# Conditioning product in eight halves of four column tiles over the first four feed-forward chunks, and loops over one chunk

## The chip, the cores and the metric

The kernel runs on one core of one Trainium2 chip. The metric is the device time of one execution in microseconds (us), as the median of several runs. Five engines work side by side: TensorE (PE; its weight loads are shown as PEld), VectorE (DVE), ScalarE (ACT), GpSimd (POOL) and SyncE (SP), which here issues nearly all DMA loads. Each engine works off its own instructions in program order, and they wait for each other on semaphores.

## The reference

One step of a decoder layer for a prompt of 1024 tokens and 8 samples of one token each, in float32, model width 1024, feed-forward width 2816. What matters here is the conditioning product `mod` and the first feed-forward:

```python
mod = (jax.nn.silu(c) @ w_ada[l] + b_ada[l]).reshape(c.shape[0], 9, 1, D_MODEL)
h = x * (1 + mod[:, 1]) + mod[:, 0]
x = layer_norm(ALPHA * x + 0.5 * mod[:, 2] * swiglu(h, ffn1_wg[l], ffn1_wu[l], ffn1_wd[l]),
               ln_g[l, 0], ln_b[l, 0])
h = x * (1 + mod[:, 4]) + mod[:, 3]
out, k_a, v_a, k_b, v_b = mixer(l, h)
x = layer_norm(ALPHA * x + mod[:, 5] * out, ln_g[l, 1], ln_b[l, 1])
h = x * (1 + mod[:, 7]) + mod[:, 6]
x = layer_norm(ALPHA * x + 0.5 * mod[:, 8] * swiglu(h, ffn2_wg[l], ffn2_wu[l], ffn2_wd[l]),
               ln_g[l, 2], ln_b[l, 2])
```

`c` has 9 rows (one of the prompt, eight of the samples); `w_ada` is 1024 x 9216, 37.7 MB.

## The kernel before

**The two feed-forwards** each run over 11 chunks of 256 hidden columns. Tokens (1032) are in three groups `g` of 344 columns; every product is three float32r matmuls (`mm3`, L211 to L213: high times high, high times low, low times high). A chunk has an **up phase** of six units (0 to 5), each of which is gate and up for one half `j` of the chunk and one group `g`, 48 matmuls, in the order (0,0), (0,1), (0,2), (1,0), (1,1), (1,2), and a **down phase** of 24 outputs of 6 matmuls.

**Behind a unit** stand ACT's SiLU into SIL (L393), DVE's product with the up bank into GF (L427), ACT's rounded copy Ghi (L399) and POOL's remainder Glo (L472). The units share two pairs of PSUM banks: PE may start unit u when GF of unit u-2 is done (the wait on `gf_done` in `up_pe`, L348).

**Weights** come in six pieces of 0.5 MB for each chunk (two of wg, two of wu, two of wd) through three buffers RAW, fetched by SP in order (`ffn_fetch_chunk`, L305). Piece q may be fetched when piece q-3 has been split. ACT splits off the high part (`split_hi`, L309, waits for the landing) and POOL the low part (L313). ACT does this at two places of its program (`refill_after`): the next chunk's pieces 0 and 1 between unit 2's and unit 3's work, pieces 2 to 5 after unit 5.

**The conditioning product** is cut in 18 blocks of 512 columns. Blocks 0 to 3 are done before the first feed-forward, two column tiles wide (`ada4_*`). Blocks 4 to 17 are done inside it, in groups of three blocks with bases 4, 7, 10, 13 and 15 (block 15 twice). For each block 32 columns of `siluT` are the stationary operand, and the three blocks of a group go to three column tiles of 32 output rows of one PSUM bank. A group is done in two **halves** of the contraction (four of eight k tiles each). SP fetches a half as three loads of 1 MB into ADA0 to ADA2 (`ada_fetch`, L531), each after PE has done the half before (`ada_done`); `ada_pe` (L541) does 12 matmuls. After a group's second half comes its **turn**: DVE copies the bank to `modrow` (L556), PE transposes it in four pieces (L550), and DVE adds `b_ada` into `modT` (L517).

**Where the halves stand.** In `ffn_pe` a chunk with one half does it after unit 5, before the down phase; a chunk with two does the first after unit 2 and the second after unit 5. Chunk 0 has two halves (group 0, which the down phase of chunk 0 needs); chunks 1 to 8 have one each; 9 and 10 none. SP fetches them in the matching places: a half's loads stand behind the weight pieces of its chunk.

**Loops.** On PE and DVE chunks 1 to 6 are a loop (`Fori`) of three passes over a body of two chunks; 7 to 10 are written out. ACT and POOL loop over one chunk. The second feed-forward has on all engines a loop over one chunk (PE's at L1984), without conditioning.

SP also loads, behind the first half of group 1, `bias_rows` (1.5 MB) and `joint_rows` (4.5 MB).

Of the kernel before, what the change touches and what calls it, by code (L numbers as in the profile page):

```python
# [9 lines left out]
P = 128  # L10
# [11 lines left out]
CH = FT // 2  # L22
# [10 lines left out]
UNIT_D = NG * KT  # L33

F32 = mybir.dt.float32
# [79 lines left out]
def build(nc, io):  # L115

    ctx = ExitStack()
    with ctx:
        arena = Arena(nc)

        def sem(name):
            return ctx.enter_context(nc.semaphore(name))
# [24 lines left out]
        ident = arena.at("ident", [P, P], F32, off); off += 4 * P  # L147
# [28 lines left out]
        LNOFF = off  # L176
        ADA = []
        o = LNOFF
        for i in range(3):
            ADA.append(arena.at(f"ADA{i}", [P, KT // 2, 512], F32, o)); o += 2 * KT * 512  # L180
        o = LNOFF
        NT = []
# [3 lines left out]
        for g in range(NG):  # L186
# [6 lines left out]
        o = HOFF + 4 * TB * D + 4 * D + 8 * P  # L193
        ADA4 = [arena.at("ADA4_0", [P, KT, 512], F32, o), arena.at("ADA4_1", [P, KT, 512], F32, LNOFF),
                arena.at("ADA4_2", [P, KT, 512], F32, LNOFF + 16384), arena.at("ADA4_3", [P, KT, 512], F32, GOFF)]
        modrow = arena.at("modrow", [96, 512], F32, LNOFF + 32768)
        TABLES = o + 16384
        OUTT = [arena.at(f"OUTT{i}", [P, D], F32, HOFF + 4 * D * i) for i in range(4)]

# [3 lines left out]
        bank = [psum[:, i, :] for i in range(8)]  # L203
        MISC = 7
# [12 lines left out]
        x_in = [sem(f"x_in{h}") for h in range(2)]  # L217
        setup_pe, setup_act, setup_dve = sem("setup_pe"), sem("setup_act"), sem("setup_dve")
        ada4_in = [sem(f"ada4_in{i}") for i in range(4)]
        ada_in = [sem(f"ada_in{i}") for i in range(3)]  # L220
        ada_done, ada_evac, ada_turned = sem("ada_done"), sem("ada_evac"), sem("ada_turned")
        ada4_done = sem("ada4_done")
        mod_prep = sem("mod_prep")
# [29 lines left out]
        ffn = {1: FFN(1), 2: FFN(2)}  # L253
# [71 lines left out]
        def ffn_fetch_chunk(sp, x, c, slots=range(6)):  # L325
            for s in slots:
                fetch(sp, f"ffn{x.n}", x.source(2 * c, s), 6 * c + s, s % 3, 2 * c + s // 3)


        FULL = [(0, 0), (0, 1), (0, 2), (1, 0), (1, 1), (1, 2)]  # L330
# [109 lines left out]
        def ffn_dve(dve, x, r, ub, db, units, ada=(), before=None, norm=None, down0=0, done=0):  # L440

            for i in range(done, len(units)):
                if before is not None and (not done and i < NG):
                    norm_y(dve, before, i)
                gf_dve(dve, x, ub + i, i)
                if before is not None and done and i <= NG:
                    norm_y(dve, before, i - 1)
            turns = ada and ada[-1][2]
            if turns:
                ada_dve(dve, ada[-1][0])  # L450
            if len(ada) == 2:
                ada_turn_dve(dve, *ada[-1][:2])
                dve.wait_ge(ada_evac, 2 * ada[-1][0] + 7)
                prep_gate(dve, 2, 0.5)
            for g in range(len(units) // 2):
                if before is not None:
                    dve.wait_ge(ln_y, before.at(g))
                if norm is not None and g == 2:
                    center(dve, norm, 0)
                for d in range(KT):  # L460
                    v = KT * g + d
                    if norm is not None and v == 2 * KT + 4:
                        center(dve, norm, 1)
                    down_dve(dve, x, db + v, d, g, bank[4 + (down0 + v) % 3])
                    if norm is not None:
                        two_sums(dve, g, d, x.y_evac, db + v + 4)
                    if d == 2 and g == 0 and turns and len(ada) == 1:
                        ada_turn_dve(dve, *ada[-1][:2])

        def g_lo_pool(pool, x, u, i, j, g):  # L470
# [40 lines left out]
        def mod_add(dve, first, blocks):  # L511

            out = modT[:, bass.ds(4 * first, 4 * blocks), :].rearrange("p (i j) n -> p i j n", j=4)
            bias = vecT[:, bass.ds(4 * first, 4 * blocks)].rearrange("p (i j) -> p i j", j=4)
            turned = bank[MISC][:, 0:128 * blocks].rearrange("p (j i n) -> p i j n", j=4, i=blocks)[:, :, :, 0:NC1]
            for i in range(blocks):
                last = dve.tensor_tensor(out[:, i], turned[:, i], bias[:, i].unsqueeze(2).to_broadcast([P, 4, NC1]),  # L517
                                         ALU.add)
            last.then_inc(ada_evac, 1)
# [6 lines left out]

        def ada_fetch(sp, base, q, half):

            for i in range(3):
                sp.wait_ge(ada_done, 3 * q + i + 1)  # L530
                sp.dma_start(ADA[i][:, :, :], wada[:, 4 * half:4 * half + 4, bass.ds((base + i) * 512, 512)]  # L531
                             ).then_inc(ada_in[i], 16)

        def ada_pe(pe, group, base, half):
            if half == 0:
                pe.wait_ge(ada_evac, 2 * group + 5)
            for i in range(3):
                pe.wait_ge(ada_in[i], 32 * group + 16 * half + 16)
            for k in range(4):
                for i in range(3):  # L540
                    ins = pe.matmul(bank[MISC][32 * i:32 * i + 32, :], siluT[:, 4 * half + k, :], ADA[i][:, k, :],  # L541
                                    start=(half == 0 and k == 0), stop=(half == 1 and k == 3))
                    if k == 3:
                        ins.then_inc(ada_done, 1)

        def ada_turn_pe(pe, group):

            pe.wait_ge(ada_evac, 2 * group + 6)
            for j in range(4):
                last = pe.transpose(bank[MISC][:, 96 * j:96 * j + 96], modrow[:, j * P:(j + 1) * P],  # L550
                                    ident[0:96, 0:96])
            last.then_inc(ada_turned, 1)

        def ada_dve(dve, group):
            dve.wait_ge(ada_done, 6 * group + 9)
            dve.tensor_copy(modrow[:, :], bank[MISC][0:96, :]).then_inc(ada_evac, 1)  # L556

        def ada_turn_dve(dve, group, base):
            dve.wait_ge(ada_turned, group + 3)
            mod_add(dve, base, 3)  # L560

        def mod(i):
            return modT[:, i * KT:(i + 1) * KT, :]
# [1010 lines left out]
        def _(sp):  # L1574
# [26 lines left out]
            ada_fetch(sp, 4, 0, 0)  # L1601
            ada_fetch(sp, 4, 1, 1)
            ffn_fetch_chunk(sp, ffn[1], 1)
            ada_fetch(sp, 7, 2, 0)
            sp.wait_ge(bias_out, 80)
            sp.dma_start(bias_rows, bass.AP(bias_heads.tensor, 3 * NH * EXT, [[0, P], [1, NH * EXT]])).then_inc(bias_spread, 16)
            sp.dma_start(joint_rows, bass.AP(joint_heads.tensor, 0, [[0, P], [1, NH * EXTA]])).then_inc(bias_spread, 16)
            ffn_fetch_chunk(sp, ffn[1], 2)
            ada_fetch(sp, 7, 3, 1)
            with sp.Fori(2, 4) as g:  # L1610
                ffn_fetch_chunk(sp, ffn[1], 2 * g - 1)
                ada_fetch(sp, 3 * g + 4, 2 * g, 0)
                ffn_fetch_chunk(sp, ffn[1], 2 * g)
                ada_fetch(sp, 3 * g + 4, 2 * g + 1, 1)
            for half in range(2):
                ffn_fetch_chunk(sp, ffn[1], 7 + half)
                ada_fetch(sp, 15, 8 + half, half)
            with sp.Fori(9, CH) as c:
                ffn_fetch_chunk(sp, ffn[1], c)
            after_phase(sp, "proj")  # L1620
            for q in range(6):
# [190 lines left out]
        def _(dve):  # L1812
# [13 lines left out]
            for k in range(3):  # L1826
                last = dve.tensor_copy(BROWJ[:, k * EXT:(k + 1) * EXT], bank[k][0:2 * NH, 0:EXT])
# [8 lines left out]
                scaled(dve, init, g)  # L1836
                input_lo(dve, init, g)
            ffn_dve(dve, ffn[1], 0, 0, 0, FULL, ((0, 4, 0), (0, 4, 1)), before=init)
            with dve.Fori(1, 4) as g:
                ffn_dve(dve, ffn[1], 2 * g - 1, 6 * (2 * g - 1), UNIT_D * (2 * g - 1), FULL, ((g, 3 * g + 4, 0),))  # L1840
                ffn_dve(dve, ffn[1], 2 * g, 6 * (2 * g), UNIT_D * (2 * g), FULL, ((g, 3 * g + 4, 1),))
            for c in (7, 8):
                ffn_dve(dve, ffn[1], c, 6 * c, UNIT_D * c, FULL, ((4, 15, c - 7),))
            ffn_dve(dve, ffn[1], 9, 54, 9 * UNIT_D, FULL)
            dve.wait_ge(ada_evac, 15)
            prep(dve, 3, 4, 0)
            ffn_dve(dve, ffn[1], CH - 1, 6 * (CH - 1), UNIT_D * (CH - 1), FULL, norm=ln[1])
            dve.wait_ge(ffn[1].y_evac, UNIT_D * CH + 3)
# [59 lines left out]
        def _(pe):  # L1908
            for n in (1, 2):
                pe.sem_inc(ffn[n].up_done, 6)  # L1910
                pe.sem_inc(ffn[n].down_done, UNIT_D)
            pe.sem_inc(ada_done, 3)
            pe.wait_ge(const_ready, 4)
            pe.wait_ge(rows_in, 80)
            nv = MT + 6 * KT
# [4 lines left out]
            for u in range(XU):  # L1920
# [5 lines left out]
                for b in range(4):  # L1926
                    last = pe.transpose(bank[2 + u % 4][:, b * P:(b + 1) * P],
                                        XTOK[:, 4 * h + b, k * P:(k + 1) * P], ident[:, :])
# [15 lines left out]
            ada4_pe(pe, 1)  # L1944
            pe.wait_ge(bias_ev, 1)
            ffn_pe(pe, ffn[1], 0, 0, 0, FULL, ((0, 4, 0), (0, 4, 1)), fresh=True)
            with pe.Fori(1, 4) as g:
                ffn_pe(pe, ffn[1], 2 * g - 1, 6 * (2 * g - 1), UNIT_D * (2 * g - 1), FULL, ((g, 3 * g + 4, 0),))
                ffn_pe(pe, ffn[1], 2 * g, 6 * (2 * g), UNIT_D * (2 * g), FULL, ((g, 3 * g + 4, 1),))
            for c in (7, 8):  # L1950
                ffn_pe(pe, ffn[1], c, 6 * c, UNIT_D * c, FULL, ((4, 15, c - 7),))
            ffn_pe(pe, ffn[1], 9, 54, 9 * UNIT_D, FULL)
            ffn_pe(pe, ffn[1], CH - 1, 6 * (CH - 1), UNIT_D * (CH - 1), FULL, norm=ln[1])
            var_pe(pe, ln[1], 0)
            pe.wait_ge(resid_done, 1)
# [67 lines left out]
```

## Time and profile before

| | us |
|---|---|
| median of 3 runs | 2281.07 |
| the runs | 2275.48, 2281.56, 2281.07 |
| the profiled execution | 2280.34 |
| its span, first to last instruction | 2278.5 |
| PE busy | 2171.7 (95%) |
| DVE busy | 800.7 (35%) |
| POOL busy | 624.1 (27%) |
| ACT busy | 568.0 (25%) |

The chain of work that ended last, followed back from the last instruction, is PE for 87% and DVE for 7% of the span. The first feed-forward lies between about 56 and 882 us, the second between about 1468 and 2240 us. The views are of one execution; times in them count from the span's start. In a row of the timeline stand the start, the length, engine, line, operation, what is written from what, the shape, and in brackets how long the engine was idle before it and what ended that. "issue" there is idle time for which the profile shows no wait.

### The profile page before, as it was taken

The numbers are of one execution on the slowest core, as the hardware profiler recorded it, in microseconds if no ns is written. First come the engines' busy times: TensorE is split into PE (matmuls) and PEld (weight loads), VectorE is DVE, ScalarE is ACT, GpSimd is POOL, SyncE is SP. The second block draws the span as 40 slices with busy tenths as digits, with TensorE's granted clock in tenths as the row PEclk, the third lists the DMA queues.
The fourth block names the chain that finished last, engine by engine and source line by source line (L and its number), as shares of the span: only waits on it lengthen the run. The fifth ranks groups of instructions, "written<-read, shape, count | busy, mean of one in ns | idle before, by whom it ended". The sixth has DMA issues, their size and how long they took to land.

```text
span 2278.5 us, 33154 instructions
## 1 busy us (share of the span) xinstructions
PE 2171.7 (95%) x13244; PEld 1990.6 (87%) x13244; DVE 800.7 (35%) x1763; ACT 568.0 (25%) x1072; POOL 624.1 (27%) x397
## 2 busy tenths in 40 slices
PE   6999999999999999999789889989999999999996
PEld 2899999999999997998644459889999999999995
DVE  1432212321123339102455652762222212222228
ACT  2211121111111114322355550351111121111114
POOL 1422232223232230133233342132323232323210
PEclk8999999999999999999989999999999999999999
DMA  8463213222121020422442012111111111111001
GB/s 287 158 203 111 93 38 111 93 93 88 61 95 54 28 56 1 157 62 88 143 140 84 1 38 65 38 38 56 45 48 50 42 47 45 54 38 55 28 1 75
DMA packets 167775, 171.36 MB, mean 75 GB/s; under 512 B 14235, under 2 KB 130699, under 8 KB 167157
## 3 DMA queue, kind: packets, MB, share of 16 engines
q1 hardware_dynamic: 167668, 169.84, 23.0%
q8 instruction: 80, 1.31, 0.2%
q14 instruction: 27, 0.21, 0.0%
HBM read 156.91 MB, written 19.20 MB: 77 GB/s over the span
## 4 chain that ended last, share of the span: by engine, by line
PE 87%; DVE 7%; SPq 2%; ACT 2%; issue 1%; DMA 1%; POOL 0%; DVEq 0%; ACTq 0%
PE psum L211 26%; PE psum L213 25%; PE psum L212 25%; PE psum L1075 2%; PE psum L541 2%; PE psum L1134 1%; PE psum L976 1%; PE psum L639 1%; PE psum L1431 1%; SPq L494 1%; DVE NT L690 1%; DVE Hlo L703 1%; DVE RSTD L671 1%; PE psum L968 1%; DVE Y L654 1%
## 5 line engine op out<-in xcount | busy, mean ns | idle before, releaser
L211 PE MATMUL psum<-Hhi,Whi 128*128 128x344 f32 x2736 | 882.9, 323 | 26.7 <-DVE GF L427 9.9
L213 PE MATMUL psum<-Hhi,Wlo 128*128 128x344 f32 x2736 | 878.8, 321 | 0.0
L212 PE MATMUL psum<-Hlo,Whi 128*128 128x344 f32 x2736 | 878.2, 321 | 0.0
L313 POOL TENSOR_TENSOR Wlo<-RAW,Whi 128x1024 fp32r<-128x1024 f32 x158 | 393.1, 2507 | 690.4 <-ACT Whi L309 689.7
L211 PEld LDWEIGHTS psum<-Hhi,Whi 128*128 128x128 f32 x2736 | 519.2, 190 | 37.4 <-issue 22.5
L213 PEld LDWEIGHTS psum<-Hhi,Wlo 128*128 128x128 f32 x2736 | 518.9, 190 | 0.0
L212 PEld LDWEIGHTS psum<-Hlo,Whi 128*128 128x128 f32 x2736 | 518.2, 189 | 0.3
L427 DVE TENSOR_TENSOR GF<-SIL,psum 128x344 f32<-128x344 f32 x132 | 67.7, 513 | 898.3 <-ACT SIL L393 898.2
L434 DVE SCALAR_TENSOR_TENSOR Y<-psum,G,Y 128x344 f32<-128x344 f32 (+1 forms) x528 | 300.9, 572 | 181.4 <-PE psum L213 181.4
L211 PE MATMUL psum<-Ghi,Whi 128*128 128x344 f32 x1056 | 341.4, 323 | 9.8 <-DVE Y L434 5.3
L212 PE MATMUL psum<-Glo,Whi 128*128 128x344 f32 x1056 | 338.8, 321 | 0.0
L213 PE MATMUL psum<-Ghi,Wlo 128*128 128x344 f32 x1056 | 338.1, 320 | 0.0
L472 POOL TENSOR_TENSOR Glo<-GF,Ghi 128x344 fp32r<-128x344 f32 x132 | 125.8, 953 | 725.1 <-ACT Ghi L399 725.1
L309 ACT ACTIVATE Whi<-RAW 128x1024 fp32r<-128x1024 f32 x158 | 159.5, 1048 | 521.0 <-PE psum L213 461.2
L393 ACT ACTIVATE SIL<-psum 128x344 f32<-128x344 f32 x132 | 60.3, 457 | 692.0 <-PE psum L213 692.0
L211 PEld LDWEIGHTS psum<-Ghi,Whi 128*128 128x128 f32 x1056 | 198.5, 188 | 19.5 <-issue 7.5
L213 PEld LDWEIGHTS psum<-Ghi,Wlo 128*128 128x128 f32 x1056 | 199.5, 189 | 0.0
L212 PEld LDWEIGHTS psum<-Glo,Whi 128*128 128x128 f32 x1056 | 199.0, 188 | 0.4
L1075 PEld LDWEIGHTS psum<-ident,SLOT 128*128 128x128 f32 x408 | 47.8, 151 | 55.0 <-POOL SLOT L1063 29.8
L399 ACT ACTIVATE Ghi<-GF 128x344 fp32r<-128x344 f32 x132 | 65.0, 492 | 87.2 <-DVE GF L427 86.3
L1075 PE MATMUL psum<-ident,SLOT 128*128 128x128 f32 x408 | 66.7, 302 | 18.4 <-POOL SLOT L1063 10.3
L1063 POOL TENSOR_SCALAR SLOT<-SLOT,U_RDEN 128x128 f32<-128x128 f32 (+7 forms) x64 | 47.0, 748 | 82.7 <-DVE U_RDEN L1048 82.7
(196 smaller groups left out, 1309.3 us busy)
## 6 DMA issues: line engine op xcount, KB each, us to landing
ADA<-in_w_ada SPq DMA_DIRECT2D x38, 1024.0 KB, 9.2
RAW<-in_ffn_wg SPq DMA_DIRECT2D x44, 512.0 KB, 3.9
RAW<-in_ffn_wu SPq DMA_DIRECT2D x44, 512.0 KB, 3.7
RAW<-in_ffn_wd SPq DMA_DIRECT2D x44, 512.0 KB, 3.7
RAW<-in_w_in SPq DMA_DIRECT2D x36, 256.0 KB, 3.4
SK<-in_cache_a_k SPq DMA_DIRECT2D x24, 256.0 KB, 3.4
SK<-in_cache_a_v SPq DMA_DIRECT2D x24, 256.0 KB, 3.8
joint_rows<-joint_heads SPq DMA_DIRECT2D x1, 4608.0 KB, 28.0
```

Of the source, the lines that this page charges most:

```text
L211: pe.matmul(out, whi, xhi, start=first, stop=False)
L212: pe.matmul(out, whi, xlo, start=False, stop=False)
L213: return pe.matmul(out, wlo, xhi, start=False, stop=last)
L309: act.activation(Whi[slot][:, :, :], RAW[raw][:, :, :], ACT.Copy).then_inc(W[phase].hi, 1)
L313: pool.tensor_tensor(Wlo[slot][:, :, :], RAW[raw][:, :, :], Whi[slot][:, :, :].bitcast(F32), ALU.subtract).then_inc(W[phase].ready, 1)
L393: act.activation(SIL[i % 2][:, :], bank[2 * (i % 2)][:, 0:TG], ACT.Silu).then_inc(x.silu_done, 1)
L399: act.activation(Ghi[j][:, group(g)], GF[i % 2][:, :], ACT.Copy).then_inc(x.g_hi, 1)
L427: dve.tensor_tensor(GF[i % 2][:, :], SIL[i % 2][:, :], bank[2 * (i % 2) + 1][:, 0:TG], ALU.mult).then_inc(x.gf_done, 1)
L434: last = dve.scalar_tensor_tensor(Y[:, d, cols], bk[:, 0:n], G9[:, d, 0:1], Y[:, d, cols], ALU.mult, ALU.add)
L472: pool.tensor_tensor(Glo[j][:, group(g)], GF[i % 2][:, :], Ghi[j][:, group(g)].bitcast(F32), ALU.subtract).then_inc(x.g_ready, 1)
L1063: pool.tensor_scalar(s, s, U_RDEN[:, u % 3, e:e + 1], 1.0, ALU.mult, ALU.mult).then_inc(normed, 1)
L1075: last = pe.transpose(bank[4 + p % 2][:, j * P:(j + 1) * P], slot(u, e)[:, c:c + P], ident[:, :])
```

## The change

The conditioning product inside the first feed-forward is done in groups of four blocks, with bases 4, 8, 11 and 14 (blocks 11 and 14 are computed twice). A fourth buffer ADA3 is added; `modrow` and the transposes are 128 rows wide. There are four groups of two halves, 16 matmuls and four loads of 1 MB in each. All eight halves are in chunks 0 to 3, two in each chunk, so that chunks 1 to 3 have the form that only chunk 0 had. PE and DVE loop over one chunk: one loop over chunks 1 to 3 with two halves and a turn, one over chunks 4 to 9 without. SP's loops follow this. Between SP's fetch of a chunk's weight pieces and that of the next chunk's now stand both halves' loads.

```diff
-        for i in range(3):
+        for i in range(4):
             ADA.append(arena.at(f"ADA{i}", [P, KT // 2, 512], F32, o)); o += 2 * KT * 512
...
-        modrow = arena.at("modrow", [96, 512], F32, LNOFF + 32768)
+        modrow = arena.at("modrow", [P, 512], F32, LNOFF + 32768)
...
-            if len(ada) == 2:
+            if turns and isinstance(r, int) and r == 0:
+
                 ada_turn_dve(dve, *ada[-1][:2])
-                dve.wait_ge(ada_evac, 2 * ada[-1][0] + 7)
+                dve.wait_ge(ada_evac, 7)
                 prep_gate(dve, 2, 0.5)
...
-                    if d == 2 and g == 0 and turns and len(ada) == 1:
+                    if d == 2 and g == 0 and turns and not (isinstance(r, int) and r == 0):
                         ada_turn_dve(dve, *ada[-1][:2])
...
-            for i in range(3):
-                sp.wait_ge(ada_done, 3 * q + i + 1)
+            for i in range(4):
+                sp.wait_ge(ada_done, 4 * q + i + 1)
                 sp.dma_start(ADA[i][:, :, :], wada[:, 4 * half:4 * half + 4, bass.ds((base + i) * 512, 512)]
                              ).then_inc(ada_in[i], 16)
...
-            for i in range(3):
+            for i in range(4):
                 pe.wait_ge(ada_in[i], 32 * group + 16 * half + 16)
             for k in range(4):
-                for i in range(3):
+                for i in range(4):
                     ins = pe.matmul(bank[MISC][32 * i:32 * i + 32, :], siluT[:, 4 * half + k, :], ADA[i][:, k, :],
...
-                last = pe.transpose(bank[MISC][:, 96 * j:96 * j + 96], modrow[:, j * P:(j + 1) * P],
-                                    ident[0:96, 0:96])
+                last = pe.transpose(bank[MISC][:, 128 * j:128 * j + 128], modrow[:, j * P:(j + 1) * P], ident[:, :])
...
             ffn_fetch_chunk(sp, ffn[1], 1)
-            ada_fetch(sp, 7, 2, 0)
+            ada_fetch(sp, 8, 2, 0)
             sp.wait_ge(bias_out, 80)
...
-            ffn_fetch_chunk(sp, ffn[1], 2)
-            ada_fetch(sp, 7, 3, 1)
-            with sp.Fori(2, 4) as g:
-                ffn_fetch_chunk(sp, ffn[1], 2 * g - 1)
-                ada_fetch(sp, 3 * g + 4, 2 * g, 0)
-                ffn_fetch_chunk(sp, ffn[1], 2 * g)
-                ada_fetch(sp, 3 * g + 4, 2 * g + 1, 1)
-            for half in range(2):
-                ffn_fetch_chunk(sp, ffn[1], 7 + half)
-                ada_fetch(sp, 15, 8 + half, half)
-            with sp.Fori(9, CH) as c:
+            ada_fetch(sp, 8, 3, 1)
+            with sp.Fori(2, 4) as c:
+                ffn_fetch_chunk(sp, ffn[1], c)
+                ada_fetch(sp, 3 * c + 5, 2 * c, 0)
+                ada_fetch(sp, 3 * c + 5, 2 * c + 1, 1)
+            with sp.Fori(4, CH) as c:
                 ffn_fetch_chunk(sp, ffn[1], c)
...
-            with pe.Fori(1, 4) as g:
-                ffn_pe(pe, ffn[1], 2 * g - 1, 6 * (2 * g - 1), UNIT_D * (2 * g - 1), FULL, ((g, 3 * g + 4, 0),))
-                ffn_pe(pe, ffn[1], 2 * g, 6 * (2 * g), UNIT_D * (2 * g), FULL, ((g, 3 * g + 4, 1),))
-            for c in (7, 8):
-                ffn_pe(pe, ffn[1], c, 6 * c, UNIT_D * c, FULL, ((4, 15, c - 7),))
-            ffn_pe(pe, ffn[1], 9, 54, 9 * UNIT_D, FULL)
+            with pe.Fori(1, 4) as c:
+                ffn_pe(pe, ffn[1], c, 6 * c, UNIT_D * c, FULL, ((c, 3 * c + 5, 0), (c, 3 * c + 5, 1)))
+            with pe.Fori(4, CH - 1) as c:
+                ffn_pe(pe, ffn[1], c, 6 * c, UNIT_D * c, FULL)
```

DVE's loops change in the same way as PE's, and `ada_dve`, `ada_turn_dve` and `mod_add` take four blocks.

SP, from the first half of chunk 1 on, before. RAW0 and RAW1 with `wg` and `wu` are pieces 0 and 1 of chunk 2:

```order
L531 DMA ADA0_87<-in_w_ada 128x4x512
L531 DMA ADA1_88<-in_w_ada 128x4x512
L531 DMA ADA2_89<-in_w_ada 128x4x512
L1606 DMA bias_rows<-bias_heads 128x3072
L1607 DMA joint_rows<-joint_heads 128x9216
L305 DMA RAW0_56<-in_ffn1_wg 128x8x128
L305 DMA RAW1_57<-in_ffn1_wu 128x8x128
L305 DMA RAW2_58<-in_ffn1_wg 128x8x128
```

And the same place now, with the start of SP's loop over chunks 2 and 3:

```order
L1606 DMA bias_rows<-bias_heads 128x3072
L1607 DMA joint_rows<-joint_heads 128x9216
L532 DMA ADA0_87<-in_w_ada 128x4x512
L532 DMA ADA1_88<-in_w_ada 128x4x512
L532 DMA ADA2_89<-in_w_ada 128x4x512
L532 DMA ADA3_90<-in_w_ada 128x4x512
L1609 UNCONDITIONAL_BRANCH
L1609 ISA
L305 ISA
L305 DMA RAW0_56<-in_ffn1_wg 128x8x128
L304 REGISTER_ALU
L305 DMA RAW1_57<-in_ffn1_wu 128x8x128
```

The loads of chunk 1's second half, four instead of none, now stand between the bias rows and pieces 0 and 1 of chunk 2.

PE, at the end of unit 2 and the start of unit 3 (weights `Whi2_79`) in chunk 1, before:

```order
L213 MATMUL psum<-Hhi_50,Wlo1_55 128x344
L371 REGISTER_ALU
L348 REGISTER_ALU
L211 MATMUL psum<-Hhi_50,Whi2_79 128x344
L212 MATMUL psum<-Hlo_51,Whi2_79 128x344
```

And the end of the half that now stands there, with its last five matmuls of 16:

```order
L542 MATMUL psum<-ADA3_90,siluT_63 32x512
L542 MATMUL psum<-ADA0_87,siluT_63 32x512
L542 MATMUL psum<-ADA1_88,siluT_63 32x512
L542 MATMUL psum<-ADA2_89,siluT_63 32x512
L542 MATMUL psum<-ADA3_90,siluT_63 32x512
L371 REGISTER_ALU
L348 REGISTER_ALU
L211 MATMUL psum<-Hhi_50,Whi2_79 128x344
L212 MATMUL psum<-Hlo_51,Whi2_79 128x344
```

A first half has moved between units 2 and 3, where before the units followed each other.

## Rows read from the trace of the kernel before

**Rows 1.** The page, its first line and PE's busy time.
```profile
span 2278.5 us, 33154 instructions
...
PE 2171.7 (95%) x13244; PEld 1990.6 (87%) x13244; DVE 800.7 (35%) x1763; ACT 568.0 (25%) x1072; POOL 624.1 (27%) x397
```

**Rows 2.** Chain of waits, 80 to 900 us: start, length, work.
```profile
87.76 3.65 PE psum L541 x24
...
260.72 3.56 PE psum L541 x24
...
336.62 3.56 PE psum L541 x24
...
408.28 3.56 PE psum L541 x24
...
483.94 3.56 PE psum L541 x24
...
555.61 3.56 PE psum L541 x24
...
627.64 3.56 PE psum L541 x24
```

**Rows 3.** PE's loop lines: durations ns min/median/max, first and last start us.
```profile
L1947 PEldq COMPARE_BRANCH  x3: 83/3535/3692, 285.5 to 580.4; - x3
...
L1984 PEldq COMPARE_BRANCH  x9: 83/215/237, 1619.7 to 2163.0; - x9
```

**Rows 4.** Timeline of PEld, conditioning batches two tiles wide.
```profile
49.06 0.11 PEld L502 LDWEIGHTS psum<-ADA,siluT 128*32 128x32 f32 x2 [0.32 <-issue]
49.49 0.11 PEld L502 LDWEIGHTS psum<-ADA,siluT 128*32 128x32 f32 x2 [0.32 <-issue]
```

**Rows 5.** Timeline of PE; then windows: PE busy, PEclk, DMA share, GB/s.
```profile
436.90 0.42 PE L211 MATMUL psum<-Hhi,Whi 128*128 128x344 f32 x1 [1.81 <-issue]
...
1498.32 0.42 PE L211 MATMUL psum<-Hhi,Whi 128*128 128x344 f32 x1 [1.70 <-DVE GF L427]
...
437.40:440.60 3.20, 3.20 (x13) 0.51 0.18 51
1498.40:1502.00 3.60, 3.60 (x23) 1.00 0.68 199
```

**Rows 6.** DMA packets, 290 to 433 us; 1640 to 2150 us, whose only queue this is.
```profile
q8 instruction: 7, 0.11, 0.3%
...
q1 hardware_dynamic: 32430, 23.52, 15.0%
```

**Rows 7.** Timeline of ACT and PE in chunk 0.
```profile
103.59 1.06 ACT L309 ACTIVATE Whi<-RAW 128x1024 fp32r<-128x1024 f32 x1 [14.27 <-DMA RAW<-in_ffn_wg]
105.45 1.06 ACT L309 ACTIVATE Whi<-RAW 128x1024 fp32r<-128x1024 f32 x1 [0.81 <-DMA RAW<-in_ffn_wu]
106.42 0.44 ACT L393 ACTIVATE SIL<-psum 128x344 f32<-128x344 f32 x1
...
107.45 0.43 PE L211 MATMUL psum<-Hhi,Whi 128*128 128x344 f32 x1 [0.86 <-DVE GF L427]
```

**Rows 8.** SP's loads by line: chunk 0's halves, two pieces, then a loop's half.
```profile
L531 SPq DMA_DIRECT2D ADA<-in_w_ada x3: 378/505/507, 76.5 to 77.4; - x3
...
DMA to landing us min/median/max: 5.0/7.6/9.7
...
L531 SPq DMA_DIRECT2D ADA<-in_w_ada x3: 368/505/507, 91.3 to 92.3; - x3
...
DMA to landing us min/median/max: 5.0/7.3/9.5
...
L305 SPq DMA_DIRECT2D RAW<-in_ffn_wu x1: 4456/4456/4456, 93.6 to 93.6; - x1
...
DMA to landing us min/median/max: 10.7/11.2/11.8
...
DMA to landing us min/median/max: 8.2/10.2/12.3
```

More of the change, by code:

```diff
@@ L219, in build @@
         ada4_in = [sem(f"ada4_in{i}") for i in range(4)]
-        ada_in = [sem(f"ada_in{i}") for i in range(3)]
+        ada_in = [sem(f"ada_in{i}") for i in range(4)]
         ada_done, ada_evac, ada_turned = sem("ada_done"), sem("ada_evac"), sem("ada_turned")
@@ L549, in ada_turn_pe @@
             for j in range(4):
-                last = pe.transpose(bank[MISC][:, 96 * j:96 * j + 96], modrow[:, j * P:(j + 1) * P],
-                                    ident[0:96, 0:96])
+                last = pe.transpose(bank[MISC][:, 128 * j:128 * j + 128], modrow[:, j * P:(j + 1) * P], ident[:, :])
             last.then_inc(ada_turned, 1)
         def ada_dve(dve, group):
-            dve.wait_ge(ada_done, 6 * group + 9)
-            dve.tensor_copy(modrow[:, :], bank[MISC][0:96, :]).then_inc(ada_evac, 1)
+            dve.wait_ge(ada_done, 8 * group + 12)
+            dve.tensor_copy(modrow[:, :], bank[MISC]).then_inc(ada_evac, 1)
         def ada_turn_dve(dve, group, base):
             dve.wait_ge(ada_turned, group + 3)
-            mod_add(dve, base, 3)
+            mod_add(dve, base, 4)
         def mod(i):
@@ L1838, in _ @@
             ffn_dve(dve, ffn[1], 0, 0, 0, FULL, ((0, 4, 0), (0, 4, 1)), before=init)
-            with dve.Fori(1, 4) as g:
-                ffn_dve(dve, ffn[1], 2 * g - 1, 6 * (2 * g - 1), UNIT_D * (2 * g - 1), FULL, ((g, 3 * g + 4, 0),))
-                ffn_dve(dve, ffn[1], 2 * g, 6 * (2 * g), UNIT_D * (2 * g), FULL, ((g, 3 * g + 4, 1),))
-            for c in (7, 8):
-                ffn_dve(dve, ffn[1], c, 6 * c, UNIT_D * c, FULL, ((4, 15, c - 7),))
-            ffn_dve(dve, ffn[1], 9, 54, 9 * UNIT_D, FULL)
-            dve.wait_ge(ada_evac, 15)
+            with dve.Fori(1, 4) as c:
+                ffn_dve(dve, ffn[1], c, 6 * c, UNIT_D * c, FULL, ((c, 3 * c + 5, 0), (c, 3 * c + 5, 1)))
+            with dve.Fori(4, CH - 1) as c:
+                ffn_dve(dve, ffn[1], c, 6 * c, UNIT_D * c, FULL)
+            dve.wait_ge(ada_evac, 13)
             prep(dve, 3, 4, 0)
@@ L1911, in _ @@
                 pe.sem_inc(ffn[n].down_done, UNIT_D)
-            pe.sem_inc(ada_done, 3)
+            pe.sem_inc(ada_done, 4)
             pe.wait_ge(const_ready, 4)
@@ L1946, in _ @@
             ffn_pe(pe, ffn[1], 0, 0, 0, FULL, ((0, 4, 0), (0, 4, 1)), fresh=True)
-            with pe.Fori(1, 4) as g:
-                ffn_pe(pe, ffn[1], 2 * g - 1, 6 * (2 * g - 1), UNIT_D * (2 * g - 1), FULL, ((g, 3 * g + 4, 0),))
-                ffn_pe(pe, ffn[1], 2 * g, 6 * (2 * g), UNIT_D * (2 * g), FULL, ((g, 3 * g + 4, 1),))
-            for c in (7, 8):
-                ffn_pe(pe, ffn[1], c, 6 * c, UNIT_D * c, FULL, ((4, 15, c - 7),))
-            ffn_pe(pe, ffn[1], 9, 54, 9 * UNIT_D, FULL)
+            with pe.Fori(1, 4) as c:
+                ffn_pe(pe, ffn[1], c, 6 * c, UNIT_D * c, FULL, ((c, 3 * c + 5, 0), (c, 3 * c + 5, 1)))
+            with pe.Fori(4, CH - 1) as c:
+                ffn_pe(pe, ffn[1], c, 6 * c, UNIT_D * c, FULL)
             ffn_pe(pe, ffn[1], CH - 1, 6 * (CH - 1), UNIT_D * (CH - 1), FULL, norm=ln[1])
```

## The prediction

> **What bounds the kernel now.** The page's busy times come first: PE is busy for 95% of a span of 2278.5 us [rows 1]. The profiled execution took 2280.34 us, 1.8 us more than its span; the median of the runs is 2281.07 us, 0.7 us above it. I make the sum against 2280.34. The change lies in the first eleven-chunk feed-forward, so the next view is the chain of waits there. The conditioning pieces (L541) sit in it at a regular distance [rows 2], and that gives every price of a chunk. From 483.94 to 555.61 lies a chunk with one conditioning half: 71.67 us. From 555.61 to 627.64 lies one that also turns a group: 72.03 us. From 260.72 to 336.62 and from 408.28 to 483.94 lie a turn and the jump back of the loop over two chunks: 75.90 and 75.66 us. The second feed-forward, whose loop body is one plain chunk, has eight jumps in 2163.0 - 1619.7 us [rows 3]: 67.91 us a chunk. So on PE's path **a half costs 71.67 - 67.91 = 3.76 us, a turn 0.36 us, a jump of the two-chunk loop 3.87 and 3.63 us**. In these chunks PE waits for nobody; what the other engines do costs nothing until it makes PE wait.
>
> **What the change does to the halves.** Before, ten halves with three column tiles each; after, eight with four. In one batch, the matmuls for all tiles start within some nanoseconds, and the next batch follows after 0.43 us. Two tiles wide, the batches stand at 49.06 and 49.49 [rows 4]; three wide, eight batches take 3.56 us, 0.44 us each [rows 2]. Width cost nothing between two and three, so I take it as free at four: a half stays at 3.76 us. Two halves and one turn fewer: 2 x 3.76 + 0.36 = **-7.9 us**. The upper bound is a fourth tile that costs a third of a batch, 0.14 us in each of 64 batches, 9.2 us. The 128-wide copy of modrow and the fourth addition to modT lie on DVE, for which PE waits only in chunk 0's turn; I take 0.1 us there and nothing in the others, whose 0.36 us is the price of a turn with three additions.
>
> **The jumps.** PE's branch at L1947 (body of two chunks) took 3.5 and 3.7 us when taken, the one at L1984 (body of one chunk) 0.2 us [rows 3]. The first makes PE idle for 1.8 us and then costs clock: after 1.81 us of idle time before 436.90 the granted clock was 0.51 (1.2 GHz) for 3.2 us; after 1.70 us before 1498.32 it stayed at 1.00 (2.4 GHz) [rows 5]. So 3.63 - 1.81, about **1.8 us, is what a drop of the clock costs**. I take the same for the other jump. The DMA view says why the jumps differ: while the two-chunk loop ran, instruction packets were loaded (7 in 143 us), while the one-chunk loop ran, none [rows 6]. The new loop's body has 432 matmuls and 32 for the conditioning plus 4 transposes, near the 432 of the cheap body and far from the 892 of the dear one. I take it as cheap. It has two jumps, the plain loop behind it five cheap ones. The two dear jumps go: **-7.5 us**; bounds 0 and -7.5.
>
> The Trainium skill (Runtime: NRT & Kernel Launch, Instruction fetch mechanics) says that a taken branch whose target is outside a window of two 256-instruction pages stops for a fetch. By that rule all seven jumps of the new loops would cost like the two of before. The cheap branch at L1984 jumps over a body of 864 weight loads and matmuls, more than two such pages, so the trace disagrees.
>
> **What the change does to the queue of loads.** This is what decides. In each of chunks 0 to 3 both halves are done, the first after up unit 2, the second after unit 5. Both use the same buffers, so SP waits for PE's first half before it issues the second half's four loads, and the first two weight pieces of the next chunk stand behind them. ACT is to split those two pieces after unit 2, in program order ahead of the SiLU of unit 3, and PE's unit 5 needs the bank that this SiLU and GF free. Before, only chunk 0 is like this, and the trace shows the result: ACT idle for 14.27 us until the first piece, then the second piece, the split from 105.45, the SiLU at 106.42, and PE's unit 5 at 107.45 after 0.86 us idle [rows 7]. The loads: issued from 91.3 us, the first landed after 5.0 us, the third (issued at 92.3) after 9.5, so one megabyte takes (92.3 + 9.5 - 91.3 - 5.0) / 2 = 2.7 us; the second piece landed at 93.6 + 11.8 = 105.4 us [rows 8], just when ACT starts on it. A fourth tile puts 2.7 us more ahead of it. PE then idles 0.86 + 2.7 = 3.6 us before unit 5, and such a gap brings the clock drop: 1.8 us.
> - Chunk 0: 2.7 + 1.8 = 4.5 us (its 0.86 is in the time before).
> - Chunks 1 to 3: 3 x (3.6 + 1.8) = 16.2 us.
> - The first half of chunk 0: its third tile landed at 77.4 + 9.7 = 87.1 us [rows 8], PE came at 87.76 [rows 2]. The fourth lands at 89.8: 2.1 us idle, and 1.8 us for the clock: 3.9 us.
> - In chunks 2 and 3 the loads are issued in SP's loop, with registers. There a first load landed after 8.2 us instead of 5.0 [rows 8]; that one had a weight piece ahead of it, others did not suffer as much. Bounds 0 and 3.2 us each; I take 1: 2.0 us.
>
> Together **+26.6 us**. The rest is covered. 432 matmuls in 71.67 - 3.56 us are 0.158 us each, so an up unit of 48 takes 7.6 us and a down phase of 144 takes 22.7. The first halves of chunks 1 to 3 are loaded from early in the down phase before, over 40 us ahead of their use, and four loads need 5.0 + 3 x 2.7 = 13.1 us. The second halves have three units, 22.7 us, for the same. The 6.1 MB of bias rows, issued behind the first half of chunk 1, need 17 us at that rate (double that would still end before the second half is asked for).
>
> **Sum.** -7.9 - 7.5 + 26.6 + 0.1 = +11.3 us. Since the two clock prices of chunk 0 may overlap with the slow stretch the start already has, I take off half a microsecond: +10.8, or 2291 us.
>
> **Rivals.**
> - *The jumps stay dear.* The new body is 8% longer than the cheap one. If it no longer fits, two jumps cost 3.75 us each: 2298.5 us. For it: nothing in the trace lies between 432 and 892 matmuls. Against: the distances.
> - *No clock drop.* If the five new gaps leave the clock at 1.00, 5 x 1.8 us fall away: 2282 us, within 0.3%, which is what a measurement of this kernel can tell from no change. For it: the 1.70 us gap did not; against: all five come out longer than 2 us.
> - *Faster: the weight pieces don't queue.* If the transfers ran side by side, so that the two pieces landed within 12 us of the first issue, unit 5 would start on time in all four chunks. That takes away 4 x 5.4 and the 2.0: 2267.5 us. It decides from about 13 us on: unit 5 was due at 107.45 - 0.86 = 106.6, 15.3 us after the first issue, and starts 2.1 us after the landing. Against: the landings came one after the other in the order of issue [rows 8].
> - *The fourth tile isn't free*: 9.2 us, 2300 us.
> - *Every jump stops PE*, the page's rule as a mechanism of this kernel: five jumps more at 3.75 us, and the two stay, so 7 x 3.75 = 26.3 us: 2317 us. The trace speaks against it by eight cheap jumps.
>
> **Chances.** The forecast as costed 0.67, and about 0.05 of that lies under 2288 us; dear jumps 0.10; no clock drop 0.12; faster 0.07; fourth tile 0.03; every jump 0.01. Slower by over 0.3%: 0.62 + 0.10 + 0.03 + 0.01 = 0.76; within: 0.12 + 0.05 = 0.17; faster: 0.07. The range takes in the forecast, the dear jumps and the case without clock drop, with 2 us for errors of the terms: 2280 to 2301.
>
> **What would show it.** In the profile after: four waits of PE's L211 for DVE's GF of about 3.6 us, one in each of chunks 0 to 3, each behind an ACT wait of 15 to 18 us for a weight piece; a clock of 0.50 for some 3 us after each; a wait of about 2 us for the conditioning load at 88 us; taken branches of 0.2 us and no wait of L211 for "issue"; 3.56 us for each of eight conditioning pieces. Waits under 2 us, or landings of the second piece under 15 us from the first issue, make the prediction wrong towards no change or faster; branches of 3.5 us towards slower.

## The result, and the profile after

The changed kernel takes 2290.49 us (median of 6 runs, 2289.3 to 2294.0), the kernel before 2277.6 us on the same chips. The ratio is 1.0064 (95% interval 1.005 to 1.0078): 0.64% slower. Timed again beside others it was 1.0068 (1.0054 to 1.0082). The forecast was 2291 us. One run of two_chunk_body below (2689.0 us at a mean granted clock of 0.75) and one of the kernel before in a later group (3057.4 us at 0.65) stand apart as slow runs, and medians and ratios here are without them.

PE's waits in the first feed-forward: who waited for whom, total, times, longest. The kernel before, 90 to 850 us, all lines:

```profile
PE psum L211 <- issue: 3.8, 2, 2.0
PE psum L211 <- DVE Y L434: 2.4, 2, 1.5
PE psum L211 <- DVE GF L427: 0.9, 1, 0.9
```

The changed kernel, 60 to 850 us, all lines:

```profile
PE psum L211 <- DVE GF L427: 20.5, 5, 5.5
PE psum L542 <- DMA ADA<-in_w_ada: 1.7, 1, 1.7
PE psum L211 <- DVE Y L434: 1.6, 1, 1.6
```

The waits for "issue" of before are gone. Of the five waits for GF one (5.5 us) is at 80.0 us, before unit 2 of chunk 0, where a wait of 4.3 us stood before too; the other four stand before unit 5, one in each of chunks 0 to 3. The one in chunk 0 was 0.86 us before [rows 7], the other three are new. ACT and PE in chunk 1, in the same place of the chunk as [rows 7]:

```profile
193.73 1.06 ACT L309 ACTIVATE Whi<-RAW 128x1024 fp32r<-128x1024 f32 x1 [17.21 <-DMA RAW<-in_ffn_wg]
195.60 1.06 ACT L309 ACTIVATE Whi<-RAW 128x1024 fp32r<-128x1024 f32 x1 [0.81 <-DMA RAW<-in_ffn_wu]
196.56 0.44 ACT L393 ACTIVATE SIL<-psum 128x344 f32<-128x344 f32 x1
...
197.60 0.66 PE L211 MATMUL psum<-Hhi,Whi 128*128 128x344 f32 x1 [3.79 <-DVE GF L427]
```

ACT waits 17.21 us for the first weight piece of chunk 2, splits the second as soon as it lands, and PE has idled 3.79 us when GF frees the bank. The loads in front of it, as in [rows 8]: the four of the second half, then the landing of the second piece, issued at 182.9.

```profile
L532 SPq DMA_DIRECT2D ADA<-in_w_ada x4: 373/506/805, 178.5 to 180.1; - x4
...
DMA to landing us min/median/max: 5.1/8.6/11.8
...
DMA to landing us min/median/max: 12.6/12.6/12.6
```

The fourth lands at 180.1 + 11.8 = 191.9, the second piece at 195.5, 17.0 us after the first issue. PE's clock behind the four waits and behind the wait for the conditioning load at 91.64 (windows: length, PE busy, number of matmuls, then PEclk, the mean granted clock, 1.00 for 2.4 GHz and 0.50 for 1.2 GHz; then DMA share, GB/s):

```profile
114.30:117.50 3.20, 3.20 (x15) 0.68 0.75 183
197.70:200.90 3.20, 3.20 (x12) 0.52 0.73 183
279.00:282.20 3.20, 3.20 (x12) 0.55 0.68 174
360.40:363.60 3.20, 3.20 (x14) 0.63 0.62 177
91.70:95.00 3.30, 3.30 (x32) 1.00 0.02 5
```

Each of the first four windows holds a stretch at 1.2 GHz, the last does not. The chain of waits gives the distance between a chunk's two halves, here chunk 1's:

```profile
174.96 3.69 PE psum L542 x32
...
206.83 3.57 PE psum L542 x32
```

31.87 us from start to start, 3.57 of it the half: 28.3 us for three up units, which take 22.7 us undisturbed. The rest is 3.8 us of idle time and 1.8 us of lower clock. The 32 records of a half's 16 matmuls take 3.57 us, against 3.56 us for 24 in [rows 2]. PE's branches are cheap in both new loops, L1940 with and L1942 without conditioning:

```profile
L1940 PEldq COMPARE_BRANCH  x3: 76/213/248, 231.7 to 394.6; - x3
...
L1942 PEldq COMPARE_BRANCH  x6: 76/208/219, 462.5 to 802.1; - x6
```

### The profile page after: what moved, and what is told of

It reads as the page before. It is cut to its first block, busy times and chain, and to the rows that moved or that the text cites. A ratio compares the mean times of both kernels' runs of the same rounds, so it can differ in the third digit from the quotient of the medians.

```text
span 2287.4 us, 33460 instructions
## 1 busy us (share of the span) xinstructions
PE 2166.6 (95%) x13256; PEld 1989.4 (87%) x13256; DVE 802.8 (35%) x1763; ACT 568.3 (25%) x1072; POOL 619.7 (27%) x397
## 4 chain that ended last, share of the span: by engine, by line
PE 83%; DVE 7%; DMA 3%; SPq 2%; ACT 2%; issue 1%; POOL 0%; DVEq 0%; ACTq 0%
PE psum L211 24%; PE psum L213 24%; PE psum L212 24%; DMA RAW<-in_ffn_wu 2%; PE psum L1075 2%; PE psum L1134 1%; PE psum L542 1%; PE psum L976 1%; PE psum L639 1%; DMA ADA<-in_w_ada 1%; PE psum L1431 1%; SPq L305 1%; SPq L495 1%; DVE NT L690 1%; DVE Hlo L703 1%
## 5 line engine op out<-in xcount | busy, mean ns | idle before, releaser
L211 PEld LDWEIGHTS psum<-Ghi,Whi 128*128 128x128 f32 x1056 | 198.0, 187 | 15.5 <-DVE Y L434 6.2
L399 ACT ACTIVATE Ghi<-GF 128x344 fp32r<-128x344 f32 x132 | 65.0, 493 | 87.2 <-DVE GF L427 86.3
```

The costliest lines, as they stand in the source:

```text
L211: pe.matmul(out, whi, xhi, start=first, stop=False)
L399: act.activation(Ghi[j][:, group(g)], GF[i % 2][:, :], ACT.Copy).then_inc(x.g_hi, 1)
```

## The experiments

**Theory.** The price is one of place in a queue: a second half's loads stand ahead of the two weight pieces that ACT needs, and PE waits for the bank behind ACT. **Rivals**: the volume of loads in the first four chunks; two halves in one chunk as such; the width. For the gain, the question is what a jump costs. The stretches from the first up matmul to the start of chunk 10, in us by trace, and the runs:

| kernel | chunk 0 | chunks 1-9 | median | ratio to before (95%) |
|---|---|---|---|---|
| before, first profile | 87.5 | 650.2 | | |
| before_again | 88.6 | 646.6 | 2277.9 (1 run) | |
| changed | 94.4 | 651.7 | 2290.5 | 1.0064 (1.005-1.0078) |
| after_again | 94.7 | 652.2 | 2292.8 | 1.0068 (1.0054-1.0082) |
| pieces_first | 89.1 | 635.2 | 2268.1 | 0.9964 (0.9952-0.9977) |
| pieces_first_again | 89.3 | 635.2 | 2267.9 | 0.9962 (0.9947-0.9977) |
| three_loads_ahead | 90.2 | 639.3 | 2275.2 | 0.9993 (0.9984-1.0002) |
| three_wide | 88.4 | 652.2 | 2282.7 | 1.0022 (1.0012-1.0032) |
| three_wide_first | 87.0 | 642.8 | 2270.8 | 0.9961 (0.9949-0.9974) |
| two_chunk_body | 94.5 | 656.2 | 2292.6 | 1.0078 (1.0065-1.0091) |
| before_written_out | 88.4 | 642.7 | 2273.2 | 0.9976 (0.9965-0.9987) |
| early_tile | 86.7 | 635.2 | 2267.6 | 0.9948 (0.993-0.9967) |
| early_tile_again | 87.2 | 635.2 | 2269.2 | 0.9963 (0.9949-0.9976) |

### The order of the loads

The edit in SP's loop over chunks 2 and 3; chunks 0 and 1, which are written out, and the loop behind it change alike:

```diff
             with sp.Fori(2, 4) as c:
-                ffn_fetch_chunk(sp, ffn[1], c)
+                ffn_fetch_chunk(sp, ffn[1], c, range(3, 6))
                 ada_fetch(sp, 3 * c + 5, 2 * c, 0)
+                ffn_fetch_chunk(sp, ffn[1], c + 1, range(3))
                 ada_fetch(sp, 3 * c + 5, 2 * c + 1, 1)
```

> The changed kernel with SP's order alone altered: the first three weight pieces of the next chunk are fetched ahead of the second conditioning half's four loads, in chunks 0 to 3. Theory (place in the queue): the second half's loads stand ahead of the pieces that ACT needs, and PE loses 28.3 - 22.7 = 5.6 us between the two halves of each of four chunks. With the pieces first, both waits for GF and drops of the clock go: 22.7 us between the halves, 22.5 us less, about 2268 us against 2290.5, ratio to the kernel before about 0.996. Rival (volume): 11 MB in a chunk are too much for the loads, whatever their order; then the waits only move, to the conditioning loads or to a later unit, and the time stays within 5 us of 2290.

Measured 2268.12 us. PE's waits from 85 to 830 us:

```profile
PE psum L542 <- DMA ADA<-in_w_ada: 1.8, 1, 1.8
PE psum L211 <- DVE Y L434: 1.6, 1, 1.6
```

No wait for GF is left. The halves of chunk 1 start at

```profile
170.62 3.57 PE psum L542 x32
197.02 3.57 PE psum L542 x32
```

26.4 us apart instead of 31.87. The same loads in the same chunks, in another order: the volume is not the cause, nor is it that a chunk has two halves.

The next kernel, also against the changed one, again in the loop:

```diff
-                ada_fetch(sp, 3 * c + 5, 2 * c + 1, 1)
+                ada_fetch(sp, 3 * c + 5, 2 * c + 1, 1, range(3))
+                ffn_fetch_chunk(sp, ffn[1], c + 1, range(2))
+                ada_fetch(sp, 3 * c + 5, 2 * c + 1, 1, range(3, 4))
```

> The changed kernel with the fourth load of each second half issued behind weight pieces 0 and 1 of the next chunk instead of ahead of them. Theory (place in the queue, 2.7 us a load): PE's wait before unit 5 falls from 3.9 to about 1.1 us, and the clock no longer drops behind it: 23.9 us between the halves, as chunk 0 has it in the kernel before; 4 x 4.4 = 17.6 us less, about 2273 us. If the clock drop did not hang on the length of the wait, only 4 x 2.7 = 11 us would go, 2279.5 us. Rival (volume): no change from 2290.

Measured 2275.19 us. In chunk 1 PE idles 0.97 us, and the granted clock of the 3.2 us behind it is 1.00:

```profile
192.21 0.42 PE L211 MATMUL psum<-Hhi,Whi 128*128 128x344 f32 x1 [0.97 <-DVE GF L427]
```

Between the halves lie 24.1, 24.1, 24.3 and 24.2 us. One load fewer ahead of the pieces takes away some 2.7 us of wait and 1.5 us of clock, and the two parts of the price are seen apart.

### The width and the place, each alone

From the kernel before: one-chunk loops, base `3 * c + 4`, both halves in chunks 0 to 4, ADA and the product three wide.

> The loops and places of the changed kernel without its width: five groups of three tiles, bases 4, 7, 10, 13, 15, both halves of a group in each of chunks 0 to 4, loop bodies of one chunk (1 to 3 with conditioning, 5 to 9 without). Against the kernel before: the two dear jumps go (-7.5 us); chunks 1 to 4 get the wait that chunk 0 has, with three loads ahead of the pieces, 23.9 instead of 22.7 us between the halves (+1.3 us each, +5.2): ratio 0.999, about 2275 us, 15 us less than the changed kernel. Rival (it is the two halves in one chunk as such that cost 5.6 us, however many loads they have): 4 x 5.6 - 7.5 = +15 us, ratio 1.0065.

Measured 2282.67 us, 7.7 us more than expected, though far under the rival's 2291. Chunks 0, 2 and 3 have 24.2, 24.3 and 24.1 us between the halves. Chunks 1 and 4 have 26.9 and 25.3. In chunk 1 the landings of the three loads and PE's idle time were

```profile
DMA to landing us min/median/max: 5.0/8.6/10.8
...
190.21 0.42 PE L211 MATMUL psum<-Hhi,Whi 128*128 128x344 f32 x1 [2.22 <-DVE GF L427]
```

The second landed after 8.6 us where [rows 8] have 7.3; everything behind it is 1.3 us later, the idle time grows to 2.22 us, and the clock behind it is 0.60. In chunk 4, where a load was late too, PE idles 2.26 us, and the clock stays at 1.00. With a wait near 1 us a late load costs little more than itself; near 2 us it can cost the clock too. Why a load of 1 MB now and then takes some 4 us instead of 2.7 is open. The two late loads cost 2.7 and 1.2 us of chunk time; the jumps' gain was also smaller than expected (below).

> Three tiles wide, five groups in chunks 0 to 4, one-chunk loops, and the first three weight pieces of the next chunk ahead of each second half's loads. Against the changed kernel with the pieces first, this undoes the width alone. Theory (a half costs 3.6 to 3.8 us whatever its width): two halves and a turn more, +7.9 us, and no wait for a fourth load in chunk 0, -1.8 us: 6 us slower than the one with pieces first, ratio to before 0.999. Rival (the fourth tile has a price elsewhere, such as longer turns or more load traffic): less than 3 us slower.

Measured 2270.76 us. Chunks 0 to 9 take 729.8 us, against 724.3 with four tiles: 5.5 us more, as expected, so the width does gain its two halves and the turn. In the runs the two can't be told apart (0.9961 and 0.9964): see what stays open.

### The jumps

The changed kernel with another loop on PE:

```diff
-            with pe.Fori(4, CH - 1) as c:
-                ffn_pe(pe, ffn[1], c, 6 * c, UNIT_D * c, FULL)
+            with pe.Fori(2, 5) as g:
+                for h in range(2):
+                    ffn_pe(pe, ffn[1], 2 * g + h, 6 * (2 * g + h), UNIT_D * (2 * g + h), FULL)
```

> The changed kernel with PE's plain loop over chunks 4 to 9 as three passes over a body of two chunks instead of six over one; no conditioning in that body, 864 matmuls. Theory (a jump over a body that is too long to be kept makes PE stop and drops its clock): two dear jumps, 3.5 us each as a branch, 3.75 us each on the path: plus 7.5 us, 2298 us, and instruction packets again during the loop. Rival (it was the conditioning or its register waits in the body that made the jump dear, not the length): 2290.5 us and branches of 0.2 us.

Its branches, its instruction packets from 400 to 800 us, the idle time before a jump's first matmul and the window behind it:

```profile
L1942 PEldq COMPARE_BRANCH  x3: 79/3319/3536, 530.2 to 805.8; - x3
...
q8 instruction: 25, 0.41, 0.4%
...
671.68 0.42 PE L211 MATMUL psum<-Hhi,Whi 128*128 128x344 f32 x1 [1.80 <-issue]
...
671.80:675.00 3.20, 3.20 (x21) 1.00 0.09 20
```

A plain body of 864 matmuls makes the branch dear again and has instructions loaded again (25 packets, 4 in the changed kernel): it is the length. But the clock stays at 1.00 behind both jumps. They cost 1.85 and 2.1 us instead of 3.75, 4 us together instead of 7.5. The runs don't separate this kernel from the changed one (1.0078 and 1.0064, with intervals that overlap); the reading rests on the trace.

And the kernel before with PE's loop written out:

```diff
-            with pe.Fori(1, 4) as g:
+            for g in range(1, 4):
```

> The kernel before with PE's loop over chunks 1 to 6 written out, nothing else. Theory (two jumps over the two-chunk body cost 3.87 and 3.63 us): 7.5 us less in chunks 1 to 9, ratio 0.9967, about 2269 us. Rival (the jumps cost only their idle time, and the clock would drop there or elsewhere anyway): 3.8 us less, ratio 0.9983.

Ratio 0.9976, 5.5 us less (3 to 8): between the two expectations. By trace, chunks 1 to 9 take 7.5 us less than in the first profile of before. The second profile of before shows why both sizes turn up.

> The kernel before, profiled a second time. The chunks 0 to 9 of the changed kernel take 8.4 us more than in the first profile of before, while the ratio of the runs says 12 to 18 us. Theory (the first profile of before has by chance a short start and a short second feed-forward): this profile has its first feed-forward matmul later than 56.2 us (57 to 59 us, as all the others) and the stretch from the second feed-forward's chunk 1 to the end longer than 724.9 us (726 to 727), while chunks 0 to 9 again take 737.7 us within 1 us. Rival (the change makes these other stretches longer): again 56.2 and 724.9 us within 0.5 us.

Half of this fell. The last stretch took 727.0 us (725.0 to 728.0 in the other runs); the first matmul stands at 56.8 us, hardly later than 56.2 and earlier than the 57.0 to 59.4 of the others; and chunks 0 to 9 took 735.2 us, not 737.7. The chain of waits over the first jump, and the idle time and the clock at it:

```profile
262.41 3.56 PE psum L541 x24
336.32 3.56 PE psum L541 x24
...
290.82 0.42 PE L211 MATMUL psum<-Hhi,Whi 128*128 128x344 f32 x1 [1.59 <-issue]
...
290.90:294.10 3.20, 3.20 (x21) 1.00 0.05 14
```

73.91 us, where [rows 2] have 75.90. The same kernel, the same jump, and in one execution the clock drops and in the other not. A jump costs 1.9 to 2.1 us without the drop and 3.6 to 3.9 us with it.

### Sizes once more, and a kernel that beats both

> The changed kernel once more, timed beside the kernel before. Chunks 0 to 9 took 746.1 us in it, and in the kernel before 737.7 us where the clock dropped behind both jumps and 735.1 us where it did not. Theory (waits of 3.9 us always drop the clock, the jumps' gaps of 1.8 to 2.0 us only in some executions): chunks 0 to 9 again within 1 us of 746.1, 28.3 to 28.7 us between the halves in all four chunks, ratio 1.0037 to 1.0055. Rival (the drop behind 3.9 us is as uncertain as behind 2 us): one or more chunks with 26.6 us between the halves.

Between the halves 28.4, 28.1, 28.6 and 28.8 us, chunks 0 to 9 in 747.0 us: the drop behind a wait of 3.65 us or more came in all twelve cases (the changed kernel twice, two_chunk_body). The distances lie up to 0.2 us outside the 28.3 to 28.7 expected, and the ratio, 1.0068, lies above what was expected.

> The changed kernel with three weight pieces ahead of each second half's loads, on the same chip as the two others of this group. Theory: 22.8 us between the halves in all four chunks, the wait of 1.8 us for the fourth load of chunk 0's first half, 22 us less than the changed kernel, ratio to before 0.9955 to 0.997. Rival (part of the 22 us seen before came from another stretch): 18 us or less.

Chunks 0 to 9 in 724.5 us, 22.5 less than in after_again, ratio 0.9962.

The last kernel has the pieces first and, against pieces_first:

```diff
+            sp.wait_ge(ada4_done, 2)
+            ada_fetch(sp, 4, 0, 0, range(3, 4))
             sp.wait_ge(ln_lo, init.k_at(NG - 1, KT - 1))
-            ada_fetch(sp, 4, 0, 0)
+            ada_fetch(sp, 4, 0, 0, range(3))
```

> The changed kernel with the pieces first, and the fourth load of chunk 0's first half issued ahead of SP's wait for the first layer input, since its buffer is free by then. Theory (PE waits 1.7 to 1.8 us in chunk 0 for this load alone): the wait of L542 for the load goes, 1.8 us less than with the pieces first, about 2266 us, ratio 0.9956. Rival (another load or the units' own wait ends last there): no change against the pieces first.

> Pieces first and the fourth load of chunk 0 issued early, on the same chip. Theory: no wait of PE for a conditioning load, chunk 0 in 86.7 us, 2 us less than with the pieces first alone, ratio 0.995 to 0.996. Rival (the 2.4 us that chunk 0 gained are given back before the end): same time as with the pieces first.

PE's wait for the load is gone, and chunk 0 is 2.1 to 2.4 us shorter in both pairs of traces. The runs of one chip don't show it (2269.21 against 2267.85 us, in runs that spread over 4 to 6 us). The fetch order is what makes the changed kernel faster than the kernel before, by 0.4%; whether the early load adds to it can't be told from these runs.

## Why the prediction was right

**Halves and turn (-7.9 us).** Right. A half of four tiles takes 3.57 us, and undoing the width costs 5.5 us of chunk time beside a wait of 1.8 us that it saves: 7.3.

**Waits in the four chunks (4.5 + 16.2 us).** The step that decided was right in place and size: idle times of 3.65, 3.79, 3.72 and 3.74 us for 3.6 expected, each with the clock drop, and 22 us of chunk time gone when the order alone was changed. Against the kernel before, whose chunk 0 had 1.1 us of it already, that is 20.9 us for 20.7.

**First half of chunk 0 (3.9 us).** Half right. The idle time was 1.7 us for 2.1, but the clock stayed at 1.00: the term was 2.2 us too large.

**Loads issued in SP's loop (2.0 us).** Too large. There the first load of a second half landed after 5.0 us, as outside the loop, and the second pieces 16.8 us after the first issue. Chunks 2 and 3 are less than 0.1 us longer than chunk 1 in the first profile; in after_again they are 0.5 and 0.6 us longer, with idle times of 4.02 and 4.15 us. So the term is 0.1 to 1.1 us, and the registers don't delay a landing. That the 8.2 us of [rows 8] came from the weight piece in front is likely, but not tried alone.

**Jumps (-7.5 us).** The mechanism was right: the branches fell to 0.2 us, the plain long body brought them back. The size was too large, since it was read from one execution in which the clock dropped behind both jumps. By before_again it is 3.9 us, by the runs of before_written_out 5.5 us (3 to 8). The Trainium skill's window of two pages (Runtime: NRT & Kernel Launch, Instruction fetch mechanics), taken for PE, would have made all jumps dear; the branches at L1940 and L1942, 0.2 us, contradict it.

So two terms were too dear and one too large a gain, and they cancel: the chunks took 8.4 us more than in the first profile of before and 11.0 to 11.8 more than in the second, for 10.8 forecast. The forecast also started from an execution of 2280.34 us, 2.7 us above the median that the kernel before has now. The hit to half a microsecond is luck. **What stays open:** the ratios say 14.6 us (11 to 18) and 15.5 us (12 to 19), some 3 us more than the chunks explain; the medians by themselves lie 12.9 and 16.0 us apart. The kernels with four tiles all come out 1 to 5 us above what their chunks say against before_again, those with three do not. The rest of the span outside chunks 0 to 9 differs from trace to trace by up to 9 us (1536.0 to 1545.1), and the median of the kernel before by 3 us from one group of runs to another, so I can't place it.

## What to carry to other kernels

Before moving a load, ask what stands behind it in the issuing engine's program, not only whether the load itself is in time: here one conditioning load was late, by 1.7 us in chunk 0, and the weight pieces behind such loads were late in all four chunks. When a transfer has to wait for an engine's progress, issue first those behind it that need not wait. PE's idle 3.7 us cost 5.5 us with the clock here, so one load less in front gained 4.2 us and not only 2.7.

## What the runs showed of the hardware that I had not expected

- The clock drop behind a gap of about 2 us isn't certain: behind idle times of 1.81, 2.03 and 2.22 us the clock fell, behind 1.59, 1.71, 1.80, 2.26 and, before a conditioning half, 1.4 to 1.9 us it did not. It isn't certain at 3 us either: PE's wait for GF in the first chunk of the second feed-forward, 3.0 to 3.1 us long in all 13 traces, left the clock at 1.00 in three of them (three_wide, three_loads_ahead, early_tile) and at 0.50 to 0.61 in ten. Behind waits for GF of 3.65 us and more it always fell. A price read from one execution can be off by 1.8 us for each such gap.
- PE's taken branch costs 0.2 us over a body of 468 matmuls as over one of 432, and 3.3 to 3.7 us over 864 or 892, with and without conditioning in it.
- Column tiles of a float32 matmul of 512 columns ran four wide in the time of two: a batch each 0.43 to 0.45 us.
